# A two-layer hybrid encoder step on one core: step sizes on four column groups, convolved chunks turned later, an earlier gate, and the norm's high part on ScalarE

## The reference, cut to what matters

```python
x = x + 0.5 * swiglu(rms_norm(x, g0), ...)      # d_model 1024, d_ff 2816
x = x + mixer(rms_norm(x, g1))                  # layer 0: retention || stick-breaking
x = x + 0.5 * swiglu(rms_norm(x, g2), ...)      # layer 1: band attention || Mamba-2 SSD
```

```python
xbc, conv_new = causal_conv(xbc, conv_buf, conv_w, conv_b)
dt = softplus(dt + dt_bias);  a = -exp(a_log)
y, ssm_new = ssd(xs, dt, a, bm, cm, ssm_state)   # chunked scan
y = rms_norm((y + d_skip * xs) * silu(z), ssd_gain)
```

## Time and profile before

| | us |
|---|---|
| median of 3 runs (lowest, highest) | 2261.25 (2260.23, 2261.54) |
| the profiled execution, its own time | 2263.39 |
| its span, first to last instruction | 2261.6 |
| mean granted clock of TensorE | 0.991 of full speed |
| busy: TensorE, VectorE, ScalarE, GpSimd | 2199.8, 1077.8, 324.2, 1175.5 |

### The profile page before, as it was taken

How to read it: one execution, slowest core, us unless ns; L and a number is a source line. 1 busy time by engine, 2 the same in 40 slices (tenths; PEclk the granted TensorE clock), 3 DMA queues, 4 the chain that set the end, 5 groups by cost and what they waited for, 6 DMA issues and landing times.

```text
span 2261.6 us, 40474 instructions
## 1 busy us (share of the span) xinstructions
PE 2199.8 (97%) x17187; PEld 2141.4 (95%) x17187; DVE 1077.8 (48%) x1180; ACT 324.2 (14%) x456; POOL 1175.5 (52%) x646
## 2 busy tenths in 40 slices
PE   8999999999999999999999999999989999999997
PEld 7999999998878999999999999999988789999997
DVE  5441446443747542244754314463966674413433
ACT  2100000101362210000021000002222321100001
POOL 4665656553314566556555655654533256655563
PEclk9999999999999999999999999999999999999998
DMA  4222222221111222222232222222211222222231
GB/s 173 92 96 71 84 100 95 76 96 57 52 39 67 92 74 102 74 93 97 79 112 93 102 74 86 95 89 86 80 38 48 82 85 83 107 72 91 81 114 40
DMA packets 30311, 190.43 MB, mean 84 GB/s; under 512 B 3744, under 2 KB 4128, under 8 KB 11680
## 3 DMA queue, kind: packets, MB, share of 16 engines
q1 hardware_dynamic: 23904, 173.62, 21.4%
q10 hardware_dynamic: 6336, 15.81, 1.9%
HBM read 181.91 MB, written 7.50 MB: 84 GB/s over the span
## 4 chain that ended last, share of the span: by engine, by line
PE 91%; DVE 6%; issue 1%; ACT 1%; DMA 1%; POOL 0%; ACTq 0%; DVEq 0%; POOLq 0%
PE ps L417 75%; PE ps L430 7%; PE ps L677 1%; DVE u L1408 1%; DVE cacc L1786 1%; DVE ssum L1421 1%; DVE rstd L1425 1%; DVE x L1434 1%; PE ps L987 1%; PE ps L1033 0%; PE ps L711 0%; PE ps L588 0%; PE ps L743 0%; PE ps L1013 0%; PE ps L608 0%
## 5 line engine op out<-in xcount | busy, mean ns | idle before, releaser
L417 PE MATMUL ps<-u,wh 128*128 128x272 f32 x6464 | 1080.1, 289 | 11.2 <-issue 5.6
L417 PEld LDWEIGHTS ps<-u,wh 128*128 128x128 f32 x6464 | 917.3, 188 | 13.5 <-issue 6.9
L386 POOL TENSOR_SCALAR wh<-wraw 128x1024 fp32r<-128x1024 f32 (+2 forms) x321 | 348.5, 1086 | 1030.5 <-PE ps L417 746.6
L389 POOL TENSOR_TENSOR wl<-wraw,wh 128x1024 fp32r<-128x1024 f32 (+2 forms) x321 | 826.8, 2576 | 26.7
L417 PE MATMUL ps<-u,wl 128*128 128x272 f32 x3232 | 669.0, 288 | 0.0
L417 PE MATMUL ps<-a,wh 128*128 128x272 f32 x3072 | 511.5, 288 | 1.1 <-issue 1.0
L417 PEld LDWEIGHTS ps<-u,wl 128*128 128x128 f32 x3232 | 504.8, 188 | 0.0
L417 PEld LDWEIGHTS ps<-a,wh 128*128 128x128 f32 x3072 | 435.3, 188 | 2.4 <-issue 1.8
L1450 DVE TENSOR_TENSOR tg<-ps,rstd 128x544 f32<-128x544 f32 x194 | 140.3, 724 | 593.3 <-PE ps L417 585.9
L417 PE MATMUL ps<-a,wl 128*128 128x272 f32 x1536 | 317.5, 288 | 0.0
L417 PEld LDWEIGHTS ps<-a,wl 128*128 128x128 f32 x1536 | 239.5, 188 | 0.0
(11 more groups left out here) (248 smaller groups left out, 1240.1 us busy)
## 6 DMA issues: line engine op xcount, KB each, us to landing
wraw<-in_wf_in SPq DMA_DIRECT2D x87, 1024.0 KB, 4.8
wraw<-in_wf_out SPq DMA_DIRECT2D x32, 1408.0 KB, 5.8
wraw<-in_w_ab SPq DMA_DIRECT2D x12, 1024.0 KB, 4.8
wraw<-in_w_cd SPq DMA_DIRECT2D x10, 1024.0 KB, 4.8
wraw<-in_w_abo SPq DMA_DIRECT2D x8, 512.0 KB, 3.3
wraw<-in_w_cdo SPq DMA_DIRECT2D x8, 512.0 KB, 3.3
out_y<-yout ACTq DMA_DIRECT2D x8, 272.0 KB, 2.1
bt<-in_bias ACTq DMA_DIRECT2D x1, 2048.0 KB, 8.2
```

Of the source, the lines that this page charges most:

```text
L386: nc.gpsimd.tensor_scalar(wh[:, s, 0:K * P], raw, 1.0, 1.0, ALU.mult, ALU.mult).then_inc(w_high, 1)
L389: nc.gpsimd.tensor_tensor(wl[:, s, 0:K * P], raw, wh[:, s, 0:K * P].bitcast(F32), ALU.subtract).then_inc(w_split[s], 1)
L417: last = nc.tensor.matmul(bank(b0 + 2 * s + half, 0, HT), w[:, s, k * P:(k + 1) * P], act_t[:, k0 + k, part, half * HT:(half + 1) * HT], s ...
```

## The change

Four things.

1. The step sizes leave the weight pipeline. Their 8 columns for each of 8 row chunks, padded to 32, are loaded unsplit by ScalarE's queue (`dtw`, 128 x 264 numbers); VectorE puts the norm's gain on them. TensorE multiplies them in float32 by the raw `x`: row chunk k goes to column group k mod 4 (32 output partitions), two chunks added in each group. VectorE scales the 128 partitions by 1/rms, and a second product with a 0/1 matrix sums the four groups. VectorE adds the bias behind convolution 0. The `lone` stage and its special cases in the loaders and splitters are gone.
2. Convolved chunk c-2, not c-1, is turned after product c; the last value turn comes after the first convolution product; the step sizes are turned after product 6. ScalarE copies a turned chunk one round later.
3. At t = 1 `ssd_gate(0)` stands ahead of `ssd_inputs(2)`.
4. In `residual`'s norms (all but the first of the kernel) ScalarE writes the high part, ahead of the square; VectorE adds the squares of chunk m-1 before it makes the low part.

```diff
         dtr = place("dtr", [T], F32, sil_at)
+        dtw = place("dtw", [DC * 32 + SSD_H], F32, a_at + 4 * SC)
+        dtp = place("dtp", [T], F32, a_at + 4 * SC + 1088)
         hl = place("hl", [SSD_H, P], F32, ssum_at)
...
             if f == 2:
-                stages += [(ins["w_bv"], 2, DC), (ins["w_dt"], 1, DC), (ins["w_cd"], 10, DC),
+                stages += [(ins["w_bv"], 2, DC), (ins["w_cd"], 10, DC),
                            (ins["w_cdo"][0], DC // 2, DC // 2), (ins["w_cdo"][1], DC // 2, DC // 2)]
         STAGE = {}
-        pairs, slot = 0, [0, 0]
+        pairs = 0
         for n, (arr, count, K) in enumerate(stages):
-            lone = arr is ins["w_dt"]
-            STAGE[n] = (pairs, slot[0], slot[1], count, K, lone)
+            STAGE[n] = (pairs, pairs, pairs, count, K)
             pairs += count
-            slot = [slot[0] + count, slot[1] + (0 if lone else count)]
-        FFN_STAGE = [0, 7, 11, 20]
-        AB_IN, AB_RET, AB_OUT, CD_V, CD_DT, CD_IN, CD_SSD, CD_OUT = 4, 5, 6, 15, 16, 17, 18, 19
+        FFN_STAGE = [0, 7, 11, 19]
+        AB_IN, AB_RET, AB_OUT, CD_V, CD_IN, CD_SSD, CD_OUT = 4, 5, 6, 15, 16, 17, 18
         BAND = [(c, t) for c in range(3) for t in range(TILES)] + [(3, TILES)] + [(3, t) for t in range(TILES)]
...
             for n, (arr, count, K) in enumerate(stages):
-                width = (1 if lone else 2) * K * P
                 def load(i, par_, *_):
-                    sp.dma_start(wraw[:, par_, 0:width], arr[i]).then_inc(raw_loaded[par_], 16)
+                    sp.dma_start(wraw[:, par_, 0:2 * K * P], arr[i]).then_inc(raw_loaded[par_], 16)
                 def load_after(i, par_, *_):
...
             turn_value(0, 1, 10)
-            product(0, STAGE[CD_DT][1], DC, u, None, 0)
+            pe.wait_ge(dtw_ready, 1)
+            for half in range(2):
+                for k in range(DC):
+                    g = 32 * (k % 4)
+                    last = nc.tensor.matmul(bank(4 + half, 0, HT, g, g + 32), dtw[:, k * 32:(k + 1) * 32],
+                                            x[:, k, half * HT:(half + 1) * HT], start=(k < 4), stop=(k >= 4))
+            last.then_inc(dt_part, 1)
+            product(0, STAGE[CD_IN][1], DC, u, None, 0)
             turn_value(1, 1, 11)
-
-            def turn_conv(s, c):
-
-                turn_chunk(tg[:, s, :], 12 + c, conv_src, c + 1)
-
-            product(0, c0, DC, u, None, 0)
+
+            def turn_conv(c):
+
+                turn_chunk(tg[:, c % 2, :], 12 + c, conv_src, c + 1)
+
+            pe.wait_ge(dt_scaled, 1)
+            for half in range(2):
+                last = nc.tensor.matmul(bank(4 + half, 0, HT, 0, SSD_H), dtw[:, DC * 32:DC * 32 + SSD_H],
+                                        dtp[:, half * HT:(half + 1) * HT], start=True, stop=True)
+            last.then_inc(dt_sum, 1)
             for c in range(1, 8):
                 product(c % 2, (c0, c1)[c % 2] + c // 2, DC, u, None, 0)
-                if c < 7:
-                    turn_conv((c - 1) % 2, c - 1)
-            pe.wait_ge(dt_ready, 1)
-            pe.wait_ge(tp_free, 18)
-            for t in range(5):
-                n = P if t < TILES else LS
-                last = nc.tensor.transpose(bank(6, 40 * t, 40 * t + 40, 0, n), dtda[0:40, t * P:t * P + n],
-                                           C(C_ID, 40, 0, 40))
-            last.then_inc(dtn_done, 1)
+                if c >= 2:
+                    turn_conv(c - 2)
+                if c == 6:
+                    pe.wait_ge(dt_ready, 1)
+                    for t in range(5):
+                        n = P if t < TILES else LS
+                        last = nc.tensor.transpose(bank(5, 40 * t, 40 * t + 40, 0, n), dtda[0:40, t * P:t * P + n],
+                                                   C(C_ID, 40, 0, 40))
+                    last.then_inc(dtn_done, 1)
             chunks = [(s, p_) for p_ in range(4, 10) for s in range(2)]
...
                     pe.wait_ge(evac[0], c0 + 5)
+                    pe.wait_ge(tp_free, 18)
                 if t in (0, TILES):
...
                 for m in range(DC):
-                    square(n, m, lambda: act.wait_ge(evac[m % 2], (c0, c1)[m % 2] + m // 2 + 1))
+                    act.wait_ge(evac[m % 2], (c0, c1)[m % 2] + m // 2 + 1)
+                    if n < NORMS - 1:
+                        nc.scalar.activation(u[:, m, 0, :], x[:, m, :], ACT.Identity,
+                                             scale=par[:, P_NORM + 8 * n + m:P_NORM + 8 * n + m + 1]).then_inc(u_high, 1)
+                    square(n, m, lambda: None)
             def ffn(f, n):
...
             act.dma_start(cs[:], ins["conv"]).then_inc(cdc_loaded, 16)
+            act.dma_start(dtw[:], ins["w_dt"]).then_inc(cdc_loaded, 16)
             for c in range(4):
...
                     nc.scalar.activation(dst[:, LP:T], cacc[:, LP + 3:LP + 3 + LS], ACT.Silu).then_inc(conv_src, 1)
-                    take_turned(xs_n if c < 4 else b_n, (c % 4) * P)
                     if c >= 4:
+                        act.wait_ge(conv_src, c + 1)
                         nc.scalar.copy(bc_t[:, c - 4, :], dst).then_inc(conv_out, 1)
                     nc.scalar.activation(dst[:, LP:T], cacc[:, LP + 3:LP + 3 + LS], ACT.Silu).then_inc(conv_out, 1)
+                if 1 <= c < 7:
+                    take_turned(xs_n if c < 5 else b_n, ((c - 1) % 4) * P)
             act.dma_start(outs["conv"], cnew[:]).then_inc(conv_left, 16)
...
                 g = par[:, P_NORM + 8 * n + m:P_NORM + 8 * n + m + 1]
-                V.tensor_scalar(u[:, m, 0, :], x[:, m, :], g, None, ALU.mult).then_inc(u_high, 1)
+                if n == 0:
+                    V.tensor_scalar(u[:, m, 0, :], x[:, m, :], g, None, ALU.mult).then_inc(u_high, 1)
                 dve.wait_ge(u_high, DC * n + m + 1)
...
                         dve.wait_ge(evac[s], c)
+                        if m:
+                            add_squares(n, m - 1)
                         if n < NORMS - 1:
                             norm_chunk(n, m)
-                        if m:
-                            add_squares(n, m - 1)
                 if n is not None:
...
             inv_rms(4)
+            dve.wait_ge(cdc_loaded, 32)
+            dtw3 = dtw[:, 0:DC * 32].rearrange("p (k h) -> p k h", k=DC)
+            V.tensor_tensor(dtw3, dtw3, par[:, P_NORM + 8 * 4:P_NORM + 8 * 5].unsqueeze(2).broadcast_to([P, DC, 32]),
+                            ALU.mult).then_inc(dtw_ready, 1)
             values(0, 4, 8, 2)
-            cdt = STAGE[CD_DT][1] + 1
-            dve.wait_ge(cdc_loaded, 16)
-            scaled(0, cdt, dtr[0:8, :], rows=8)
-            dve.wait_ge(evac[0], cdt)
-            V.tensor_scalar(dtr[0:8, :], dtr[0:8, :], par[0:8, P_DTB:P_DTB + 1], None, ALU.add).then_inc(dt_evac, 1)
+            dve.wait_ge(dt_part, 1)
+            V.tensor_tensor(halves(dtp[:]), pair(4), halves(rstd[:]), ALU.mult).then_inc(dt_scaled, 1)
             V.memset(xpad[:, :, 0:3], 0.0)
...
                 last.then_inc(conv_acc, 1)
+                if c == 0:
+                    dve.wait_ge(dt_sum, 1)
+                    V.tensor_scalar(halves(dtr[0:SSD_H, :]), ps[0:SSD_H, 4:6, 0:HT], par[0:8, P_DTB:P_DTB + 1], None,
+                                    ALU.add).then_inc(dt_evac, 1)
+                if c == 6:
+                    dve.wait_ge(dtn_done, 1)
+                    V.tensor_copy(dtn[:, 0:TILES, :], bank(5, 0, 160).rearrange("p (t c) -> p t c", t=TILES))
+                    V.tensor_copy(dtn[0:LS, 4, :], bank(5, 160, 200, 0, LS)).then_inc(dtn_ready, 1)
                 if c == 2:
...
             part_evac(0)
-            dve.wait_ge(dtn_done, 1)
-            V.tensor_copy(dtn[:, 0:TILES, :], bank(6, 0, 160).rearrange("p (t c) -> p t c", t=TILES))
-            V.tensor_copy(dtn[0:LS, 4, :], bank(6, 160, 200, 0, LS)).then_inc(dtn_ready, 1)
             dve.wait_ge(dtn_ready, 1)
...
                 part_evac(3 * t + 5)
+                if t == 1:
+                    dve.wait_ge(z_silu, 4)
+                    ssd_gate(0)
                 ssd_inputs(t + 1)
...
                     link(V.memset(bqz[:], 0.0))
-                if t == 1:
-                    dve.wait_ge(z_silu, 4)
-                    ssd_gate(0)
                 if t:
...
     wcd = f(w_in_cd)[0]
-    w_dt = np.zeros((D, P), np.float32)
-    w_dt[:, 0:SSD_H] = wcd[:, 24 * P:]
+    w_dt = np.zeros((P, DC * 32 + SSD_H), np.float32)
+    w_dt[:, 0:DC * 32].reshape(P, DC, 32)[:, :, 0:SSD_H] = wcd[:, 24 * P:].reshape(DC, P, SSD_H).transpose(1, 0, 2)
+    w_dt[:, DC * 32:] = np.arange(P)[:, None] % 32 == np.arange(SSD_H)[None]
     wcdo = f(w_out_cd)[0].reshape(2, 512, D)[::-1]
```

More of the change, by code:

```diff
@@ L312, in pairs_loop @@
         def pairs_loop(eng, n, body):
-            first, _, _, count, _, _ = STAGE[n]
+            first, _, _, count, _ = STAGE[n]
             if count >= 2:
@@ L351, in _ @@
                     load_after(count - 1, (count - 1) % 2)
-                elif n == CD_IN:
```

(17 more changed lines are left out.)

46 lines of the change are left out of this document (23 added, 23 removed).

## The result

The changed kernel takes 2238.85 us (median of 4 runs, 2238.73 to 2241.06), the kernel before 2261.26 (4 runs beside them): a ratio of 0.9904, 95% interval 0.989 to 0.9919. Forecast were 2236.3 us and 25.0 us less; measured are 22.4 less by the medians and 22.3 by the two profiled spans (2239.3 and 2261.6). The case that came about is the forecast one.

The account below looks back on a forecast made before the run. TensorE, busy 97% of the span, was taken to bound the kernel. Gains of 8.3 (step sizes, convolutions), 9.3 (gate), 7.1 (short boundaries) and 0.3 (long ones) made 25.0 off 2261.25: 2236.3 us, range 2227 to 2250.

Parts of the forecast that it names:

- T0: End of the first convolution product at the second mixer's entry, 1577.1 before; claimed to come 9.85 us earlier.
- first gate: State-space chunks: chunk 0's gate moved earlier removes 6.39 us of TensorE idle and 2.90 of slow running, gain 9.3.
- two short boundaries and the long ones: Norm's high part on ScalarE: gains 3.6 and 3.5 us at the K = 4 boundaries, 0.3 for all K = 11 ones.
- rival (b): Step-size products: the four column groups run one after the other, T0 5.6 us later, 2241.9; 10%.
- with four, half of that: Step-size products: four column groups take half the two-group time of 4.05 us, so 2.0 for all 16.
- T0 + 17 + 39.9 + 0.4 = T0 + 57.3: Convolutions: VectorE's chain from convolution 2's start decides the third half product's time, against T0 + 56.6 before.
- Rival (a): Convolutions: VectorE does not decide, its GpSimd collisions fall out better; gain 12.4 instead of 8.3, 2232.2; 15%.
- even chance: Convolutions: about even odds that TensorE's wait of some 3 us brings a clock loss; 0.8 us taken off.
- Rival (c): Short boundaries do not gain, as ScalarE waits and GpSimd meetings eat it; 7.1 us less gain, 2243.4; 13%.
- under 1 us: Sign at the K = 4 boundaries: TensorE's wait before the next stage this short, with GpSimd named.
- over 8 us: Sign in the convolutions: the forecast is wrong if any chunk takes this long on VectorE.
- Rival (d): Convolutions: extra VectorE-GpSimd meetings and clock losses cost 34 us against 25, making the kernel slower, 2270; 5%.

Follow-up runs that it names:

- one_group: Changed kernel with all 16 step-size products on one column group, summed over 32 rows; these products took 7.52 us against 2.04.
- short_split: Changed kernel with GpSimd splitting only 64 columns per weight block in convolutions and first blocks; step sizes and convolutions took 83.83 us, 7.2 below the changed kernel.
- bias_early: Changed kernel with VectorE's step-size bias ahead of convolution 0's passes instead of behind them; median 2239.02 us.
- silu_first: Changed kernel with ScalarE's step-size work behind the first Silu instead of ahead of the convolution loop; median 2238.29 us.
- best: Changed kernel with early bias, first Silu ahead of step-size work, earlier first half-product evacuation, and small state copies on ScalarE; 2235.19 us against 2241.07.
- norm_back: Changed kernel with the norm's high part on VectorE again and sums of squares behind the low part; 6.5 us more than the changed kernel's repeat, by medians.
- high_back: Changed kernel with the norm's high part on VectorE again, new order of sums of squares kept; the two short-boundary stretches got 2.95 and 2.98 us longer.
- after_again: The changed kernel run again without edit; its stretches behind the attention stage repeated, step sizes and convolutions taking 91.16 us.

## Why the prediction was right, and where it was off

By the two traces, with the forecast beside it:

```
                                           forecast  measured
T0 earlier (step sizes, weights' split)       9.85      9.42
T0 to the third half product                 -0.7      -2.74
clock behind TensorE's wait there            -0.8      -1.36
first gate                                    9.3       9.35
two short boundaries and the long ones        7.4       6.48
start, attention stage, last sums             0         1.17
sum                                          25.0      22.3
```

So the total is off by 2.7, with the convolutions 2.6 below the forecast together with their clock. The 1.17 are outside the change: that they were positive in this pair of profiles is luck, and without them the change's own gain is 21.1.

- *T0.* Right in mechanism and nearly in size (1576.90 to 1564.08, less the 3.40 by which the reciprocal at this entry came earlier: 1540.51 and 1537.11): the products in 2.04 us for 2.0, no idle ahead of the product, and the 1.8 of slow clock gone with the gap. one_group shows the rival (b) as a price: it would have cost 5.5. The last part of the forecast for 16 products, "with four, half of that", holds; the estimate that I drew from the Trainium skill, "TensorE: Matmul & The Clock Gate", 2.5 us, is above the measured 2.04: 7.52 / 2.04 = 3.7 times, not 3.07, which the page has for four tiles along the rows. The drain at a change of tiling mode (the Trainium skill, "TensorEngine Tiling (Array Packing)", Key Properties) cannot be told apart in this trace: the weight loads stand idle for 0.21 us ahead of 1555.98 and for 0.44 us behind the narrow products, at 1557.95, and the products themselves show no gap at either place.
- *The convolutions.* The step that failed in size: "T0 + 17 + 39.9 + 0.4 = T0 + 57.3"; measured is T0 + 59.6. The chain was the right one: Silu at T0 + 13.4 for T0 + 12.6, VectorE waiting for it 4.17, TensorE held 2.74 in the end for "some 3". The 0.8 more up to the Silu is the bias itself (0.77): the walk lets ScalarE begin where VectorE only begins the bias. And convolution 2 started at T0 + 19.1 (1583.15) instead of T0 + 17, as convolution 1's passes met the splits in full (0.56 + 5.12). The rest of the chain, up to the evacuation at 1623.18, took 40.0, for 39.9. short_split shows that these meetings, not ScalarE or the loads, set VectorE's pace, and bias_early and silu_first that the stall was worth only 2.2 to 2.7 of its 4.17. Rival (a), 12.4 if VectorE didn't decide, has the right figure for its case: C falls from 96.32 to 83.83, by 12.5, once the splits are gone, and by 12.05 in best; as the change stands it falls by 5.3.
- *The clock.* The even chance was of the right kind: of nine profiles with the same wait of 2.6 to 2.74 us, the stretch behind it ran at a granted 0.62 to 0.67 in six and at 1.00 in three (norm_back, high_back, bias_early), and C differs by 1.4 us with it.
- *The gate.* Right, 9.35 to 9.54 by three comparisons. The transposes of chunk 1 start at 1665.25 without a wait, the output products 5.19 later, for 5.16 at full clock before.
- *The boundaries.* Right in mechanism, 2.9 and 3.3 for 3.6 and 3.5, and 0.3 for the long ones together. In the first short one, B is 3.25 shorter, of which 0.36 is lost again at the restart behind it. From that boundary's own beginning the start came 0.3 later than walked and the restart 0.76: it waits 1.00 for VectorE, before 0.64, and VectorE's last two low parts took 2.84 and 2.87, which put off the last sum of squares (argued from the rows, not tried). Rival (c)'s price is what norm_back measures, 7.2 more for 7.1, or 6.5 without its slow stretch.
- *The signs.* Two of them did not come as named. TensorE's wait before the next stage at a short boundary is 1.44, with GpSimd named, for "under 1 us". And one convolution chunk, from 1583.15 to 1591.28, takes 8.12 us on VectorE, which "over 8 us" would count as the forecast being wrong; but the kernel before has such a chunk too (1591.20 to 1599.30, 8.10), so that the sign was badly chosen.
- *Not tried.* The later turns (part 2 of the change) were not taken out alone. TensorE's waits at the turns fell from 3.65 us (1.28, 0.54, 1.29 and 0.54) to 1.67 (0.83 and 0.84), but VectorE decides this stretch, so no run here says what they are worth.

Outside the change, the last sums of squares behaved differently: 2.18 us in the kernel before, 1.18 in the changed one, the two clock levels. The row of each:

```profile
2246.72 2.18 PE L443 MATMUL ps<-ssum,const 128*128 128x272 f32 x4 [2.40 <-DVE ssum L1421]
```

```profile
2225.39 1.18 PE L435 MATMUL ps<-ssum,const 128*128 128x272 f32 x4 [2.40 <-DVE ssum L1433]
```

after_again has 2.18 as well, so this 1.0 is no part of the gain, nor are the 0.95 of stretch A.

Rival (d) asked for 3.6 us more in each chunk; in the changed kernel the stretch from T0 to the third half product grew by 2.7 in all, 4.1 with the clock.

## What to carry to other kernels

Where two engines are both 90% busy, don't price a removed stall at its length: ask what the work behind it will run into, and price that from a run without the other engine's work. An operation that one later step needs (here the gate) goes ahead of everything that this step doesn't need; its gain was the same in both surroundings that were tried. When parts of an edit are to be told apart below 0.3%, cut the profiles at fixed instructions and compare stretches; the whole time mixes in stages that vary on their own.

## What the runs showed of the hardware

- Where an operation of VectorE with both ends in SBUF begins while an instruction of GpSimd's splits runs, the rounding copy as well as the subtraction, it stands until that is over, even the smallest (a 128x3 copy: 174 ns on average without splits, up to 2.03 us with them), and ends a fixed time behind it: 0.02 to 0.03 us for these copies, 0.57 to 0.59 for passes of 128x547. Those that read PSUM don't (128x272: 431 and 432 ns, with and without). Taking such copies away moves the meeting to the next operation of the kind.
- Four column groups of 32 ran 3.7 times as fast together as one group did the same products.
- ScalarE's multiply of 128x544 by a value per partition takes 0.75 us where its square takes 0.65 (0.66 in the earlier trace rows), and needs no table load (83 loads in the whole trace, before and after).
- The same idle stretch is followed by the lower clock in some executions and not in others. Ahead of the last sums, 2.40 us were followed by it in one of two profiles of the same kernel (2.18 and 1.18 us for the sums); ahead of the third half product, 2.74 us were in five of seven profiles with the same instructions there. It cost 1.0 and 1.4 us.
